# A two-part streaming-encoder kernel on one core: the top-k searches of its second part placed on one common clock

## What is computed

```
score = einsum('bqh,bqhk->bqk', wi, relu(dots)) * INDEX_SCALE
score = where(vis, score, -inf)
_, sel = top_k(score, 256)
logits = einsum('bqgrd,bqkgd->bqgrk', q, k[sel]) * ATTN_SCALE + bias
o = einsum('bqgrk,bqkgd->bqgrd', softmax(logits), v[sel])
y = x + rmsnorm(concat(pool_branch * silu(ga), o * silu(gb)) @ w_out)
```

## Time and profile before

| | us |
|---|---|
| median of 3 runs | 1634.06 (1633.37 to 1636.78) |
| the profiled execution | 1636.42 |
| its span | 1634.4 |
| PE busy | 1504.7 (92%) |
| DVE busy | 1142.1 (70%) |
| ACT busy | 889.4 (54%) |
| POOL busy | 467.6 (29%) |

### The profile page before, as it was taken

How to read it: one execution, slowest core, us unless ns; L and a number is a source line. 1 busy time by engine, 2 the same in 40 slices (tenths; PEclk the granted TensorE clock), 3 DMA queues, 4 the chain that set the end, 5 groups by cost and what they waited for, 6 DMA issues and landing times.

```text
span 1634.4 us, 17094 instructions
## 1 busy us (share of the span) xinstructions
PE 1504.7 (92%) x4935; PEld 849.2 (52%) x4935; DVE 1142.1 (70%) x2753; ACT 889.4 (54%) x1684; POOL 467.6 (29%) x387
## 2 busy tenths in 40 slices
PE   7999899999999999988888888999989998899996
PEld 4555555555555887756444444444444444454552
DVE  5412577769998556665347999999999989885312
ACT  3112333333334445552289999998889896633331
POOL 0111211121111323211333444443433433332241
PEclk9999999999999999988799999999999999999999
DMA  9322222231111110146622222221220101202111
GB/s 368 67 59 49 74 55 64 56 100 48 61 47 58 60 47 35 45 135 173 223 63 58 74 53 75 79 60 48 57 84 26 47 27 32 58 14 80 33 39 45
DMA packets 89990, 117.56 MB, mean 72 GB/s; under 512 B 16957, under 2 KB 63613, under 8 KB 89514
## 3 DMA queue, kind: packets, MB, share of 16 engines
q1 hardware_dynamic: 88666, 112.55, 22.2%
q10 hardware_dynamic: 1232, 3.93, 2.2%
HBM read 71.87 MB, written 43.54 MB: 71 GB/s over the span
## 4 chain that ended last, share of the span: by engine, by line
PE 26%; DVE 13%; ACT 7%; issue 5%; POOL 2%; POOLq 0%; ACTq 0%; DVEq 0%
PE wide L1703 9%; PE wide L1688 8%; DVE above L344 4%; ACT act_junk L1579 3%; PE bank L1663 2%; PE bank L1664 2%; PE bank L1665 2%; DVE max_junk L1768 2%; PE bank L1636 2%; POOL E L1538 1%; ACT E L1613 1%; ACT act_search L1587 1%; DVE S L379 1%; PE wide L1636 1%; DVE osb L1823 1%
## 5 line engine op out<-in xcount | busy, mean ns | idle before, releaser
L931 PE MATMUL bank<-hT,home 128*128 128x512 f32 (+2 forms) x1280 | 487.3, 517 | 5.1 <-DVE sga L1146 2.4
L1538 POOL TENSOR_TENSOR E<-E,home 128x512 f32<-128x512 f32 (+1 forms) x174 | 240.3, 1384 | 453.4 <-ACT E L1613 453.2
L931 PEld LDWEIGHTS bank<-hT,home 128*128 128x128 f32 x1280 | 235.7, 191 | 165.1 <-issue 142.8
L1688 PE MATMUL wide<-E,home 128*128 128x512 f32 x544 | 286.0, 608 | 15.1 <-POOL E L1538 15.1
L1613 ACT ACTIVATE E<-bank 128x512 f32<-128x512 f32 (+1 forms) x290 | 165.2, 570 | 198.6 <-PE bank L1665 179.2
L907 ACT ACTIVATE relu<-wide 128x1024 f32<-128x1024 f32 (+7 forms) x192 | 153.9, 802 | 213.6 <-PE wide L949 161.4
L1184 DVE SCALAR_TENSOR_TENSOR S<-relu,wi,S 128x1024 f32<-128x1024 f32 (+7 forms) x168 | 173.7, 1034 | 103.7 <-ACT relu L907 96.2
L1768 DVE CUSTOM_DVE_ANT_0 max_junk<-bank,mask 128x512 bf16<-128x512 f32 (+3 forms) x235 | 138.1, 607 | 81.6 <-PE bank L1636 61.8
L1703 PE MATMUL wide<-home 128*128 128x512 f32 x272 | 145.7, 627 | 35.7 <-ACT osb L1605 35.6
L1579 ACT ACTIVATE act_junk<-S,minus_cand 128x1152 uint8<-128x1152 f32 (+5 forms) x105 | 155.4, 1480 | 1.5
L949 PE MATMUL wide<-kiT,qiT 96*128 96x512 f32 (+3 forms) x304 | 139.4, 527 | 6.4 <-ACT relu L907 6.4
(11 more groups left out here) (216 smaller groups left out, 2231.0 us busy)
## 6 DMA issues: line engine op xcount, KB each, us to landing
xs<-x_prompt SPq DMA_DIRECT2D x16, 512.0 KB, 4.2
home<-w_in SPq DMA_DIRECT2D x16, 512.0 KB, 14.2
xr<-x_prompt SPq DMA_DIRECT2D x16, 512.0 KB, 4.2
y_prompt<-osb SPq DMA_DIRECT2D x16, 512.0 KB, 2.8
first_q<-q_high_scratch SPq DMA_DIRECT2D x24, 256.0 KB, 4.7
s_scratch<-S SPq DMA_DIRECT2D x11, 512.0 KB, 2.7
gb<-gb_scratch SPq DMA_DIRECT2D x17, 256.0 KB, 5.1
home<-ma_scratch SPq DMA_DIRECT2D x17, 256.0 KB, 5.1
```

The costliest lines, as they stand in the source:

```text
L931: mm = pe.matmul(out, stationary(c), moving(c), start=(c == 0), stop=(c == DC - 1))
L1538: pool.tensor_tensor(E[:, k % 4, :, 0:n], E[:, k % 4, :, 0:n], EB[:, kv * GRP:(kv + 1) * GRP, off:off + n], ALU.mult)\
L1688: pe.matmul(wide[0][:, kv * 512:kv * 512 + GRP * n].rearrange("p (j n) -> p j n", j=GRP), values[:, kt, kv:kv + 2, :].rearrange("p a d -> ...
```

## The change

The per-step merge is gone. `start` gives every step a place on one clock of model units (a step of n key tiles is 3.5n + 14 long), and every series of every step is placed on this clock and merged once. The searches no longer belong to steps: `search_bounds` lays them one after the other from the clock's zero, each as long as its key tiles + 3 by one common pace (the tightest that the limits allow), ACT in one interval and DVE in the next. Each tile's limit is the time of the first M that needs its mask, less `ROUND_TRIP` = 14 units. The choosing is cut into four pieces, placed singly. The mask is made in place in `B.reach`, stored off the chip and loaded back into the mask buffer, as was so for tiles 2 to 5. The SP list is put on the same clock.

```diff
+ROUND_TRIP = 14.0
...
+    start = {-1: -6.0}
+    for t in STEPS:
+        tiles = key_tiles(t) if 0 <= t < NPT else 4 if t == ST else 0
+        start[t + 1] = start[t] + 3.5 * tiles + (14.0 if 0 <= t - 2 < NT else 0.5) + (5.5 if t == -1 else 0.0)
...
+        for u in tiles:
+            size.append(size[-1] + key_tiles(u) + 3)
+        size.append(size[-1] + key_tiles(tiles[-1]) + 3)
+        limit = {i + 2: when(u - 1, maxima_from(u)) - ROUND_TRIP for i, u in enumerate(tiles)}
...
+            tight = min(ends, key=pace.get)
+            for j in range(at + 1, tight + 1):
+                bounds.append(bounds[at] + pace[tight] * (size[j] - size[at]))
+        return {u: tuple(bounds[i:i + 3]) for i, u in enumerate(tiles)}
...
+        for u, (_, a, b) in bounds.items():
+            tiles = key_tiles(u)
+            costs = [(("R", u, r), 0.155 * tiles + 0.4) for r in range(ZOOM_AT, ALL_ROUNDS)]
+            costs += [(("C", u, part), tiles * (0.25, 0.28, 0.2, 0.3)[part] + 0.3) for part in range(CHOICES)]
...
+                series.append(([item], a + (b - a) * done / whole, 0.0))
...
+            series.append((pieces, a, b))
...
+        for u, (_, _, b) in bounds.items():
+            series.append(([("MS", u)], b + 1.5, 0.0))
+            series.append(([("ML", u)], max(b + 5.0, when(u - 2, 0.0) + 0.5), 0.0))
+            if u >= FIRST + 1:
+                series.append(([("S", u)], bounds[u - 3][2] + 0.5 if u >= FIRST + 3 else start[1] + 0.1, 0.0))
...
+                    elif kind == "MS":
+                        t = at[0]
+                        n = key_tiles(t) * P
+                        sp.wait_ge(mask_ready, t - FIRST + 1)
+                        sp.dma_start(m_dram[t, :, 0:n], B.reach[:, 0:n]).then_inc(mask_out, 16)
...
-                def set_mask(u):
+                def choose_part(u, part):
                     nonlocal n
                     w = key_tiles(u) * P
-                    if u > FIRST:
-                        dve.wait_ge(mask_done, u - FIRST)
-                    n = choose(dve, dk, n, B, 0, S[sslot(u)][:, 0:w])
-                    dve.wait_ge(fl_full, last_fl(u - 3) + 1)
-                    dve.tensor_scalar(mask[:, u % 3, 0:w], B.reach[:, 0:w], MASKED, None, ALU.mult)\
-                       .then_inc(mask_done, 1)
-                    dve.memset(B.room[:], 0.0).then_inc(S_used, 1)
+                    if part == 0 and u > FIRST:
+                        dve.wait_ge(mask_out, 16 * (u - FIRST))
+                    n = choose(dve, dk, n, B, S[sslot(u)][:, 0:w], part)
+                    if part == CHOICES - 1:
+                        dve.tensor_scalar(B.reach[:, 0:w], B.reach[:, 0:w], MASKED, None, ALU.mult)\
+                           .then_inc(mask_ready, 1)
```

More of the change, by code:

```diff
@@ L355, in halve, with choose @@
     return n
-def choose(dve, done, n, B, i, s):
+CHOICES = 4
+def choose(dve, done, n, B, s, part):
     def link(ins):
@@ L1166, in _ @@
                             dve.wait_ge(m_out, 16 * (t - EARLY[0]))
-                        n = choose(dve, dve_chain, n, B, 0, Se[:, 0:w])
+                        for part in range(CHOICES):
+                            n = choose(dve, dve_chain, n, B, Se[:, 0:w], part)
                         dve.tensor_scalar(B.reach[:, 0:w], B.reach[:, 0:w], MASKED, None, ALU.mult)\
@@ L1274, in sslot, with when, search_bounds, in_order @@
         return (t - FIRST) % 3
-    def in_order(*series):
+    STEPS = range(-1, NT + 3)
+    start = {-1: -6.0}
+    for t in STEPS:
+        tiles = key_tiles(t) if 0 <= t < NPT else 4 if t == ST else 0
+        start[t + 1] = start[t] + 3.5 * tiles + (14.0 if 0 <= t - 2 < NT else 0.5) + (5.5 if t == -1 else 0.0)
+    def when(t, share):
+        return start[t] + share * (start[t + 1] - start[t])
+    def search_bounds():
+        tiles = list(range(FIRST, NT))
+        size = [0.0]
+        for u in tiles:
+            size.append(size[-1] + key_tiles(u) + 3)
+        size.append(size[-1] + key_tiles(tiles[-1]) + 3)
+        limit = {i + 2: when(u - 1, maxima_from(u)) - ROUND_TRIP for i, u in enumerate(tiles)}
+        bounds = [start[0]]
+        while len(bounds) < len(size):
+            at = len(bounds) - 1
+            ends = [j for j in limit if j > at]
+            pace = {j: (limit[j] - bounds[at]) / (size[j] - size[at]) for j in ends}
+            tight = min(ends, key=pace.get)
+            for j in range(at + 1, tight + 1):
+                bounds.append(bounds[at] + pace[tight] * (size[j] - size[at]))
+        return {u: tuple(bounds[i:i + 3]) for i, u in enumerate(tiles)}
+    bounds = search_bounds()
+    def in_order(series):
         placed = []
@@ L1292, in dve_step @@
[L1292 to L1305, removed]
+    def pe_order():
+        series = []
+        for t in STEPS:
+            if t == NT:
+                series.append(([("B",)], start[t], start[t]))
+            outs = [("O", t - 2, i, c) for i in range(2) for c in range(DC)] if 0 <= t - 2 < NT else []
+            series += [([("A", *j) for j in jobs(t)], start[t], start[t + 1]),
+                       ([("M", *m) for m in maxima_of(t + 1)], when(t, maxima_from(t + 1)), when(t, 0.78)),
+                       ([("X", t + 1)] if t + 1 < NPT else [], when(t, 0.86), 0.0),
+                       (outs[:8], when(t, 0.04), when(t, 0.46)), (outs[8:], when(t, 0.54), when(t, 0.98))]
+        return in_order(series)
@@ L1306, in act_step, with act_order @@
+    def act_order():
+        series = []
+        for t in STEPS:
+            series += [([("E", *j) for j in jobs(t)], start[t], start[t + 1]),
+                       ([("Y", t - 2, 0)] if 0 <= t - 2 < NT else [], when(t, 0.5), 0.0),
+                       ([("Y", t - 2, 1)] if 0 <= t - 2 < NT else [], when(t, 1.0), 0.0)]
+            if t == ST:
+                series.append(([("Z",)], start[t + 1], 0.0))
+        for u, (a, b, _) in bounds.items():
             pieces = [("N", u)]
@@ L1519, in _ @@
                 pool.wait_ge(eb_in, 16)
[L1520 to L1540, removed]
+                for kind, *at in pool_order():
+                    if kind == "A":
+                        mean(at[0])
+                    elif kind == "P":
+                        residual(at[0])
+                    elif kind == "V":
+                        pool.wait_ge(mask_ready, ST - 2 - FIRST + 1)
+                        pool.memset(vxs[:], 2.0).then_inc(vx_set, 1)
+                    elif near(at[0], at[2]):
+                        t, kv, kt = at
+                        k = fl[t, kv, kt]
+                        off = (place_of(t) - kt) * P
+                        pool.wait_ge(fl_free, k + 1)
+                        n = queries(t)
+                        pool.tensor_tensor(E[:, k % 4, :, 0:n], E[:, k % 4, :, 0:n],
+                                           EB[:, kv * GRP:(kv + 1) * GRP, off:off + n], ALU.mult)\
+                            .then_inc(biased, 1)
             @block.scalar
@@ L1620, in _ @@
                         while waiting:
                             take_sums(*waiting.pop(0))
+                    else:
+                        t, kv, kt = at
+                        k = fl[t, kv, kt]
+                        act.wait_ge(fl_full, k + 1)
+                        if k >= 4:
+                            act.wait_ge(pv_step, k - 3)
+                        n = queries(t)
+                        act.activation(E[:, k % 4, :, 0:n],
+                                       banks[2 + k % 2][:, 0:GRP * n].rearrange("p (j n) -> p j n", j=GRP), ACT.Exp).then_inc(fl_free, 1)
+                        while waiting and last_fl(*waiting[0]) <= k - 2:
+                            take_sums(*waiting.pop(0))
+                        if kt == key_tiles(t) - 1:
+                            waiting.append((t, kv))
```

346 lines of the change are left out of this document (179 added, 167 removed).

## The result

| | median us | runs | ratio to before (95%) |
|---|---|---|---|
| before | 1634.06 | 1633.37 to 1636.78 | |
| changed | 1626.09 | 1623.83 to 1626.64 | 0.9947 (0.9932 to 0.9961) |

The change makes the kernel about 8 us faster: the right sign and less than half of the 19 us that were forecast. The profiled span fell from 1634.4 to 1624.8 us.

What follows compares the result with a forecast made beforehand. Three engines nearly full together in part two, with DVE and ACT room at its ends. 1636.4 - 18 (steps) - 5 (stalls and clock) + 3 (early) = 1616.4, in the runs' terms 1615; range 1597 to 1646.

Steps and rivals of the forecast that it cites:

- rival A: Steps 3 to 14: vector work overfills the window of the maxima (M's), making the kernel slower, about 1645 to 1655; chance 0.2.
- the excess: Steps 3 to 14 before: 29.9 us of the trace's 665.5 that the 636 us sum of fullest engines leaves out.
- 18 us less: Steps 3 to 14: fullest-engine sum falls from 636 to 618 us, 14 of it in steps 3 to 11.
- 5 for stalls: Steps 11 to 14: 5 us gained of 11.5 us PE waits for POOL and 8.5 us of clock.
- case D: Half of PE's 29.9 us waits on ACT's copies and all stalls of steps 11 to 14 go: 1598; chance 0.15.
- The clock: Steps 11 to 14: PEclk under 1.00 in just these steps, costing 8.5 us; 1.00 there if right.
- The lockstep sum: Steps 3 to 14: largest engine inside the maxima's window plus largest outside, 658 us now against 637 before.
- Earlier start and lower rates: Searches start earlier, rates cut 5 to 12% in early steps: steps 4 to 6 down 2 to 3 us each.
- The choosing in four pieces: No more DVE work; the running sum moves to shares 0.42 to 0.56 of its step for tiles 11 to 14.
- rival B: Tiles 8 to 12: running sums meet near tiles' POOL multiplies and stall PE, up to 25 us, 1635; chance 0.1.
- The way off the chip: Mask store and load per searched tile take 11 to 13 us, hidden, with 3 us to spare.
- Early steps: Steps 0 to 2: ACT's search of tile 6 there loses 3 us (0 to 8).

Runs made afterwards that it cites:

- e3: Changed kernel with rounds and choosing pieces placed inside each tile's interval so all vector work runs at an even rate, their weights set to the trace; 1606.0 us.
- e8: Changed kernel with searches laid out from the clock's 36 (start of step 3) instead of from zero; 1652.6 us.
- e12: The evenly loaded kernel (e3) with searches laid out from the clock's 36 instead of from zero; 1628.6 us.
- e1: Changed kernel with the vector engine writing each searched tile's mask straight into its buffer, without store and load; 1629.1 us.
- e4: Kernel before with only the ScalarE part of the change: its sixteen rounds per tile laid out on the common clock from zero; 1631.4 us.

## Why the prediction was wrong

**The step that failed** is the one that put rival A aside: "PE is up to three M's ahead, a tenth of the window (5 us), so DVE can end the window late and catch up outside". By it the steps came to 618 us, and with what was left of the excess (29.9 - 5) to 643. They took 659.8. Put as a term: "18 us less" for the steps and 5 for stalls, 23 together, was 5.7. DVE did end the window late, and caught up only in part: in step 12 the stretch of the maxima grew by 12.7 us and the rest shrank by 9.9. The mechanism of A was written down with its place (52 us of vector work against 45.5 of PE in the window of step 12, an overhang of 7), and PE was idle for 7.2 us of that stretch. e3 confirms it: taking the surplus out of the window, with the same work, the same intervals and the same pieces, gives 20 us.

**Where the gain came from.** The 18 us of the forecast lie, by its own figures for the steps, all in steps 3 to 11 (the prediction says 14 there); these steps gained 1.0. What the steps did gain is step 14, where the forecast had 68 us before and after. That the sign came out right is therefore luck in part: other terms than the one that was to carry it made up for the loss.

**A's own price was not right either.** It had 1645 to 1655. Two gains came on top that I had mostly written off: PE's waits for POOL ended (12.9 of 13.6 us, forecast as 5 with the clock), and those for the copies fell by 11.3 us, which the forecast gave to case D. Against them stand 17 us more that PE waits for maxima. Two of A's signs told little: step 13 was to take over 70 us, and took 73.2 already before (71.9 now), and PE's waits for maxima were to be several times 20 us, but were 37.2. A's other sign, step 12 over 70 us, came (71.6, from 68.8).

**The clock.** The prediction says that the granted clock is under 1.00 in just the steps of the last choosings. It was 0.95 in step 3 too, and 0.92 and 0.96 in steps 4 and 5:

```profile
855.60:897.40 41.80, 35.06 (x101) 17.21 (x100) 29.42 (x90) 38.43 (x87) 17.51 (x13) 0.92 0.22 57
897.40:940.70 43.30, 37.81 (x111) 18.89 (x110) 39.91 (x101) 41.23 (x89) 20.39 (x15) 0.96 0.24 70
```

In the changed kernel these three and steps 13 and 14 are at 1.00, steps 11 and 12 still at 0.98, where 1.00 was forecast, and steps 6 and 7 fell from 1.00 to 0.96 and 0.97. No run separates what the clock gave.

**The lockstep sum as a tool.** It hits the changed kernel (658 against 659.8), but this is no proof of it: over steps 3 to 13 it gives 569, 590, 559, 610 and 580 us for before, changed, e3, e8 and e12, and the traces have 592, 593, 571, 622 and 601. It misses between 3 and 23 us, and puts e12 below the changed kernel where the trace has it above. The difference between e12 and e3, 21 us by it, was 22.5 in the medians. It finds where the surplus lies and about how large it is, not the time of a version to 10 us.

**Earlier start and lower rates.** Steps 4 to 6 were forecast 2 to 3 us shorter each; they changed by -4.1, -1.0 and +1.5 us. Steps 11 and 12 were forecast 2 us shorter and unchanged; they got longer by 2.0 and 2.8, which fits A's surplus. What the early start is worth against the kernel before no run gives: the 23 to 27 us of e8 and e12 hold for the new layout with its 14 units of reserve.

**The choosing in four pieces.** That the pieces would cost through PE's three banks was in the sum only as 15 us not gained. Shown: uncut at the new place they cost 53 us, in four pieces nothing more than in seven.

**POOL and the running sum.** Right for tiles 13 to 15 as far as PE's waits for POOL go, and rival B fell (its price for the clock, 1.7 to 3.4 us, is 1.4 to 3.7 by the prediction's own terms): the bias multiply is still held up beside the running sums of tiles 9 to 11, up to 4.06 us, but PE's only wait for it is 0.7 us.

**The way off the chip.** Right that it is hidden: e1 shows no gain without it, and no maximum of steps 3 to 14 waits for a mask load. That 3 us were to spare was not tested.

**Early steps.** I had 3 us lost. Steps 0 to 2 took 53.6 us before and 52.4 after. The search in them does cost: without it (e8) they take 48.5, so 3.9 us, near the forecast. With the old DMA list the same search costs 1.8 (e4, 55.4 against 53.6). Something else in the change gives back 5.1 (53.6 before, 48.5 in e8); the new order of the DMA list is what is left, but this was not tried alone.

**What lay outside.** Of the 9.6 us between the two profiled spans, 2.1 fell before part two begins, where the programs do the same; among all profiled runs here this start varies by some 5 us. Medians are not touched by a single such draw, but a sum made against one profile is.

## What to carry to other kernels

When two engines hand work to each other through a few buffers, compare their loads inside the stretch in which they do so, not only over the whole step: here room outside the stretch paid a surplus inside back only in part, and taking the surplus out gave 20 us of 1626. Spread background work by what the engine has left at each point, not evenly by time. Cut its long pieces, but see where that ends: four pieces of up to 5.7 us instead of one block of 9 to 15 were worth 53 to 69 us, seven pieces nothing more.

## What the runs showed of the hardware

A running sum with two inputs in the on-chip memory also takes longer behind a GpSimd addition; the prediction's rows show only the other way round. With 1792 columns it took 3.88 us before and 5.73 us in the changed kernel, where a residual addition on GpSimd had begun just ahead of it:

```profile
1244.62 2.37 POOL L1593 TENSOR_TENSOR osb<-osb,xr 128x1024 f32<-128x1024 f32 x1 [4.62 <-DVE osb L1907]
```

The addition ran for 2.0 us more after the running sum was issued at 1245.00, and the running sum took 1.85 us longer. So part of PE's 3.3 us of waiting at this place may come from GpSimd. The new order puts the norm, which releases this addition, right before the running sum of tiles 13 to 15. The addition of the choosing, by contrast, took 1.09 us at 1792 columns where it had taken 2.09 behind a bias multiply. The rule cited in the prediction (the Trainium skill, SBUF — State Buffer, "Who interferes with whom") has it for both ways: the instruction that issues first blocks the other. Both rows agree. The prediction priced only GpSimd's waits.
